# A two-layer hybrid encoder trunk: adaLN sums by one accumulating VectorE operation, a tile-by-tile prologue and transposed host layouts

## The chip, the core and the metric

The kernel runs on one core of a Trainium2 chip. The metric is the device time of one execution in microseconds (us), as the median of several runs. Engines: TensorE (PE in the profile; PEld is its weight load), VectorE (DVE), ScalarE (ACT), GpSimd (POOL), SyncE (SP, which issues most of the DMAs).

## What is computed

The sizes are 1024 tokens, model width 1024, two layers, all in fp32. Cut to what matters here:

```python
def adaln(c, w, b):                       # c (1, 1024), w (1024, 3072)
    mod = (c @ w + b)[:, None, :]
    shift, scale, gate = jnp.split(mod, 3, axis=-1)
    return shift, scale, gate

for l in range(DEPTH):
    shift, scale, gate = adaln(c, w_ada_mix[l], b_ada_mix[l])
    u = x * (1.0 + scale) + shift
    y = hybrid_mixer(u, ...)              # input projection, conv group and attention group, output projection
    x = layer_norm(DN_ALPHA * x + (1.0 + gate) * y, ln1_g[l], ln1_b[l])
    shift, scale, gate = adaln(c, w_ada_ffn[l], b_ada_ffn[l])
    u = x * (1.0 + scale) + shift
    y = conv_gated_mlp(u, ...)            # up, depthwise conv of 3 on the gate branch, SiLU, down
    x = layer_norm(DN_ALPHA * x + (1.0 + gate) * y, ln2_g[l], ln2_b[l])
```

The mixer's conv group is a gated causal depthwise convolution of 31 taps; its attention group has 8 query heads, 2 key heads and a window of two chunks of 64 tokens.

## The kernel before, in words

**Layout.** Activations lie with features on the 128 partitions and tokens along the row: `x` is 8 tiles of 128 features by 1024 tokens. The tokens are worked in two blocks of 512 (T), b = 0 and 1. Every projection is a list of slabs (`SLABS`): one slab makes 128 output features of one block of 512 tokens from 8 (or 5, 6) tiles of 128 inputs. Each fp32 product is made of three reduced-precision ones: the weights are split into `w_hi` (ACT, `split_hi`, L1163) and `w_lo` (POOL, `split_lo`, L1932, four pieces), the inputs into `u_hi` and `u_lo` (or `h_hi`, `h_lo`), and L886 to L888 issue hi x hi, hi x lo and lo x hi. A slab of 8 tiles is 24 matmuls of 512 columns. Kinds of slabs: g, a (conv group), q, k, v (attention), o (output projection), ug, uv (up: gate and value), d (down), e (the last down slabs, second half of the tokens).

**Order.** All engines walk the same list of slabs, and `plan()` hangs small steps on slabs (`STEPS[n]`): conv taps on DVE ("tap"), the attention's scores, maxima, exponentials, turns and weighing of v ("sc", "mx", "pr", "tr", "pv"), the norms ("xm" and so on), the adaLN sums ("ad", "as"), the turning of x ("xt") and of the finished half ("tm"). A planner gives every slab room for DVE steps in tenths of a microsecond (`room`, `used`) and puts the taps where room is left. Slab n's output bank is one of two PSUM banks up to slab 35, one of three from there on; it is freed by ACT or DVE. Weights are loaded four slabs ahead (`NRAW`), split three ahead (`NHI`). On DVE, a ug slab runs two gate operations (L1896, L1899), then the first background step of its list, then the tanh operation (L1905) and the rest of the list; a uv slab runs value times gate (L1912), the first step if the next slab is a ug, `h_lo` (L1919), and the rest. ACT runs, in a uv slab, `h_hi`, `split_hi` and its steps in the order of the list: "mx" makes the exponentials (L1283), "tr" the copy of the turned weights (L1299), for which PE's weighing of v ("pv", L1006) waits.

**Prologue.** x arrives with tokens on the partitions; PE turns it (`x_to_features`, L842, eight 128x128 turns for 128 tokens) and ACT copies it out (`evac_x`, L1168): four tiles before the first slab, four ("xt") behind slabs 2 to 5. The first layer's shift and scale (chunks 0 to 3 of 512 columns) are made in front of the slabs: DVE adds 7 of 8 input tiles weighted by c (`add_first`, L1464, L1467), PE adds the last one and sums over the partitions (`first_sums`, L1093, L1100), in two halves: features 0 to 511 first, then slabs 0 and 1 run over tiles 0 to 3, then the other half. `idle_products` (L1080) fill PE's gaps. POOL makes `u_lo` of tiles 0 to 3 (L2008), DVE that of tiles 4 to 7 (L1519). POOL also makes the angles of the rotary tables in two parts (`angles`, L1948 to L1958).

**adaLN sums of chunks 4 to 23.** A chunk is 512 of the 3072 columns of one of the four adaLN products; a part is a quarter of its 1024 inputs (512 KB). `load_ada` on SP loads one part a step ahead into one of two buffers, when the part before the last is used. Chunks 8, 9 and 10: DVE weights and adds (`add_ada`, L1585, L1588). All others: ACT weights (`ada_scale`, L1324, 2 operations a part) and POOL adds (L1999, L2003). Then PE sums over partitions: chunks 4 to 7 with products against ones (L1018), copied out by ACT; chunks 8 to 23 by turning four blocks (`sum_ada`, L915), reduced by DVE (L1595).

**End.** The first block's finished x is turned by PE in four steps "tm" on slabs 346 to 352 (eight turns each), copied out by ACT and DVE (L1331, L1709), and stored as rows; the second block goes through `tail_turn`, whose norm is made with tokens on the partitions.

## Time and profile before

| | |
|---|---|
| median of 3 runs | 2101.79 us (2101.77 to 2103.06) |
| the profiled execution | 2101.31 us, its span 2099.5 us |
| granted TensorE clock | 0.997 of full speed |
| busy: PE, PEld, DVE, ACT, POOL | 98%, 81%, 57%, 49%, 67% of the span |
| DMA | 250 MB, mean 119 GB/s |

How to read it: a busy share is an average over stages with different limits. Matmuls are pipelined and their ends are modelled, so matmuls overlap in the timeline: the distance from one start to the next is what one costs, and 512 columns are started every 0.227 us in the full stretch. A timeline row gives start, duration, engine, line, operation, output<-inputs, and in brackets the idle time before and what ended it.

### The profile page before, as it was taken

How to read it: one execution, taken by the hardware profiler on the slowest of the kernel's cores; microseconds unless marked ns; L12 is line 12 of the kernel's file. 1: busy time of each engine (PE TensorE's matmuls, PEld its weight loads, DVE VectorE, ACT ScalarE, POOL GpSimd, SP SyncE). 2: the span in 40 equal slices, each digit the busy share in tenths (PEclk: the TensorE clock that was granted, in tenths of full speed). 3: DMA queues.
4: the chain of work that ended last, by engine and by line, in shares of the span. 5: the costliest groups of instructions: out<-in, count | busy, mean ns of one | idle time of the engine just before them, and what ended most of it. 6: DMA issues, size and time to landing. Idle time of an engine off the chain costs nothing.

```text
span 2099.5 us, 27374 instructions
## 1 busy us (share of the span) xinstructions
PE 2064.8 (98%) x9619; PEld 1701.8 (81%) x9619; DVE 1191.1 (57%) x1940; ACT 1031.2 (49%) x1845; POOL 1413.6 (67%) x1780
## 2 busy tenths in 40 slices
PE   7999999999999999999999999999999999999997
PEld 6877778787888878888788888888878888888887
DVE  5888888675515554777632645587651455332235
ACT  3585356555516674374643756235562465333332
POOL 4987767755778887875557885564556776545454
PEclk9999999999999999999999999999999999999999
DMA  8644544533434354553233333332323332434332
GB/s 301 157 134 148 161 127 148 162 108 103 121 111 124 107 162 145 141 159 93 76 100 106 111 111 91 101 103 73 100 76 107 88 104 84 128 99 123 94 100 78
DMA packets 421510, 250.07 MB, mean 119 GB/s; under 512 B 48149, under 2 KB 393085, under 8 KB 421373
## 3 DMA queue, kind: packets, MB, share of 16 engines
q1 hardware_dynamic: 420506, 248.03, 39.8%
q8 instruction: 77, 1.26, 0.3%
q14 instruction: 60, 0.49, 0.1%
q10 hardware_dynamic: 867, 0.29, 0.1%
HBM read 242.71 MB, written 4.26 MB: 118 GB/s over the span
## 4 chain that ended last, share of the span: by engine, by line
PE 86%; POOL 5%; ACT 3%; DVE 3%; issue 2%; ACTq 0%; DMA 0%; POOLq 0%; DVEq 0%
PE fg L886 27%; PE fg L888 27%; PE fg L887 27%; POOL w_lo L1932 3%; PE bank_s L984 1%; POOL ada_acc L2003 1%; ACT ada L1324 1%; PE bank_l L915 1%; PE bank_t L993 1%; PE bank_t L1006 1%; DVE bank_c L1539 0%; POOL ssum L2030 0%; POOL u_lo L2012 0%; ACT probs L1291 0%; ACT probs L1283 0%
## 5 line engine op out<-in xcount | busy, mean ns | idle before, releaser
L1932 POOL TENSOR_TENSOR w_lo<-raw,w_hi 128x256 fp32r<-128x256 f32 (+1 forms) x1425 | 1031.3, 755 | 609.8 <-ACT w_hi L1163 608.7
L886 PE MATMUL fg<-u_hi,w_hi 128*128 128x512 f32 x2112 | 834.7, 395 | 6.2 <-DVE u_lo L1519 2.6
L888 PE MATMUL fg<-u_hi,w_lo 128*128 128x512 f32 x2112 | 823.7, 390 | 0.0
L887 PE MATMUL fg<-u_lo,w_hi 128*128 128x512 f32 x2112 | 823.5, 390 | 0.0
L1163 ACT ACTIVATE w_hi<-raw 128x1024 fp32r<-128x1024 f32 (+2 forms) x387 | 375.6, 971 | 385.6 <-PE fg L888 278.4
L886 PEld LDWEIGHTS fg<-u_hi,w_hi 128*128 128x128 f32 x2112 | 397.1, 188 | 102.5 <-issue 14.5
L888 PEld LDWEIGHTS fg<-u_hi,w_lo 128*128 128x128 f32 x2112 | 397.0, 188 | 84.2
L887 PEld LDWEIGHTS fg<-u_lo,w_hi 128*128 128x128 f32 x2112 | 397.4, 188 | 80.1 <-issue 0.5
L1539 DVE SCALAR_TENSOR_TENSOR bank_c<-glu,par,bank_c 128x512 f32<-128x512 f32 x448 | 306.1, 747 | 0.1
L1886 DVE SCALAR_TENSOR_TENSOR x<-fg,mod,x 128x512 f32<-128x512 f32 (+1 forms) x168 | 121.6, 724 | 319.3 <-PE fg L888 319.0
L888 PE MATMUL fg<-h_hi,w_lo 128*128 128x512 f32 (+1 forms) x704 | 269.8, 383 | 0.0
L886 PE MATMUL fg<-h_hi,w_hi 128*128 128x512 f32 (+1 forms) x694 | 268.4, 387 | 0.6 <-DVE h_lo L1919 0.6
L887 PE MATMUL fg<-h_lo,w_hi 128*128 128x512 f32 (+1 forms) x694 | 266.9, 385 | 0.0
L1896 DVE SCALAR_TENSOR_TENSOR fg<-gate,par,fg 128x512 f32<-128x512 f32 x88 | 66.4, 755 | 331.8 <-ACT fg L1382 331.7
L888 PEld LDWEIGHTS fg<-h_hi,w_lo 128*128 128x128 f32 x704 | 132.3, 188 | 26.0
L886 PEld LDWEIGHTS fg<-h_hi,w_hi 128*128 128x128 f32 x694 | 130.4, 188 | 26.4 <-DVE h_lo L1919 1.0
L887 PEld LDWEIGHTS fg<-h_lo,w_hi 128*128 128x128 f32 x694 | 130.4, 188 | 25.5
L1392 ACT ACTIVATE h_hi<-fg 128x512 fp32r<-128x512 f32 x88 | 52.6, 597 | 175.6 <-DVE fg L1912 175.3
L2003 POOL TENSOR_TENSOR ada_acc<-ada_acc,ada 128x512 f32<-128x512 f32 x102 | 133.2, 1305 | 5.9 <-ACT ada L1324 1.9
L1324 ACT ACTIVATE ada<-ada,ccol 128x512 f32<-128x512 f32 x136 | 90.2, 713 | 5.9 <-DMA ada<-in_w_ada_mix_dram 4.9
L1387 ACT ACTIVATE tanh_c<-fg 128x512 f32<-128x512 f32 x88 | 52.7, 599 | 66.6 <-DVE fg L1899 66.6
L1912 DVE SCALAR_TENSOR_TENSOR fg<-fg,tanh_c 128x512 f32<-128x512 f32 x88 | 61.3, 696 | 42.2 <-PE fg L888 40.3
(272 smaller groups left out, 1860.8 us busy)
## 6 DMA issues: line engine op xcount, KB each, us to landing
raw<-in_w_up_dram SPq DMA_DIRECT2D x176, 512.0 KB, 3.8
ada<-in_w_ada_ffn_dram SPq DMA_DIRECT2D x48, 512.0 KB, 4.4
raw<-in_w_down_dram SPq DMA_DIRECT2D x64, 384.0 KB, 3.5
raw<-in_w_in_dram SPq DMA_DIRECT2D x40, 512.0 KB, 4.0
raw<-in_w_down_dram SPq DMA_DIRECT2D x64, 320.0 KB, 3.1
ada<-in_w_ada_mix_dram SPq DMA_DIRECT2D x32, 512.0 KB, 4.2
raw<-in_w_in_dram SPq DMA_DIRECT2D x32, 256.0 KB, 3.7
raw<-in_w_out_dram SPq DMA_DIRECT2D x32, 256.0 KB, 2.9
```

What stands on the lines that cost most here:

```text
L886: pe.matmul(out, hi[:, k, :], rhi, start=k == order[0], stop=False)
L887: pe.matmul(out, hi[:, k, :], rlo, start=False, stop=False)
L888: ins = pe.matmul(out, lo[:, k, :], rhi, start=False, stop=k == order[-1])
L1163: act.activation(hi_of(n)[:, 0:nk, :], raw[n % NRAW][:, 0:nk, :], ACT.Copy).then_inc(hi_ready, 1)
L1324: act.activation(ada[m % 2][:, i, :], ada[m % 2][:, i, :], ACT.Copy, scale=ccol[:, k:k + 1]).then_inc(ada_mul, 1)
L1387: act.activation(tanh_c[:], ps[:], ACT.Tanh, scale=0.5).then_inc(gate_act, 1)
L1539: ins = dve.scalar_tensor_tensor(out=conv[:, j, :] if k == CONV_K - 1 else acc[:], in0=src, scalar=w, in1=acc[:], op0=ALU.mult, op1=ALU.add)
L1886: dve.scalar_tensor_tensor(out=xs(b, k)[:, cols], in0=ps[:, 0:cols.stop - cols.start], scalar=at_gate, in1=xs(b, k)[:, cols], op0=ALU.mult ...
L1896: dve.scalar_tensor_tensor(out=ps[:], in0=gate[:, 1:1 + T], scalar=par3[:, l, i + FT:i + FT + 1], in1=ps[:], op0=ALU.mult, op1=ALU.add).th ...
L1912: dve.scalar_tensor_tensor(out=ps[:], in0=ps[:], scalar=0.5, in1=tanh_c[:], op0=ALU.mult, op1=ALU.mult).then_inc(gate_dve, 1)
L1932: ins = pool.tensor_tensor(lo_of(n)[:, ks, :], raw[n % NRAW][:, ks, :], hi_of(n)[:, ks, :].bitcast(F32), ALU.subtract)
L2003: pool.tensor_tensor(acc[:], acc[:], rows[:, i, :], ALU.add).then_inc(ada_add["pool"], 1)
```

## The change

1. **Host layouts.** x comes transposed (1024 features by 1024 tokens) and is loaded straight into `x`; the first block's result is stored straight from `x` (`out_t`, features by tokens) and transposed on the host; the adaLN weights come transposed, so that 128 adaLN columns lie on the partitions and the 1024 inputs along the row (`ada_first`, `ada_t`). The turns of x ("xt", "tm"), their copies and `stage_in` are gone.
2. **c as rows.** PE spreads c over all partitions (two products against ones), ACT copies it to `c_rows` (128x1024).
3. **adaLN sums.** One 128x1024 operation with an accumulated output makes one column of `mod`, for 128 adaLN columns. First chunks: sixteen on DVE (`first_total`). Chunks 8, 9, 10 and 12 to 23: one on DVE for each part (`ada_total`). Chunks 4 to 7 and 11: POOL multiplies (`ada_weigh`, 2 operations), ACT sums in the next slab, behind its other steps ("ae"). PE's sums, ACT's and DVE's copies of them ("as") and `ada_acc` are gone.
4. **Tile-by-tile prologue.** Loads, sums, gain and bias (now on ACT), `tmp`, `u_hi` (ACT) and `u_lo` (all on POOL) go tile by tile, and slabs 0 and 1 take each tile as it comes. The idle products are gone; the taps' turns stand behind tile 5.
5. **The plan's room** is kept as it was (`used` gets the same amounts; DVE's new operations from chunk 12 on get none beyond the old reduction's), so the taps and norms stand in the same slabs.

The core of the diff:

```diff
-INSIDE = {("cm", 0): 2, ("cv", 0): 4, ("xm", 0): 4, ("xr", 0): 6,
-          ("as", 12): 2, ("as", 18): 2}
+INSIDE = {("cm", 0): 2, ("cv", 0): 4, ("xm", 0): 4, ("xr", 0): 6}
...
-DVE_CHUNKS = (8, 9, 10)
-ONES_CHUNKS = (4, 5, 6, 7)
+DVE_CHUNKS = (8, 9, 10, *range(12, 4 * NCHUNK))
...
         for part, n in enumerate(ns):
             put(n, "ad", c, part)
-            if c in DVE_CHUNKS:
+            if c in DVE_CHUNKS[0:3]:
                 used[n] += 15
-        if c in ONES_CHUNKS:
-            at(ns[-1] + 2, "as", c)
-        else:
-            put(ns[-1] + 2, "as", c)
+        for part, n in enumerate(ns):
+            if c not in DVE_CHUNKS:
+                at(n + 1, "ae", c, part)
+        if c >= DVE_CHUNKS[0]:
+            used[ns[-1] + 2] += 7
...
     for t in range(TB, TT):
-        put(t - TB + 2, "xt", t)
+        used[t - TB + 2] += 7
...
+            def load_x(b, i):
+                sp.dma_start(x[:, 2 * i:2 * i + 2, b * T:(b + 1) * T],
+                             a["x"][2 * i * P:2 * (i + 1) * P, b * T:(b + 1) * T].rearrange("(k p) n -> p k n", p=P)).then_inc(in_x[b][i], 16)
             def load_ada(m):
                 if m >= 2:
-                    sp.wait_ge(ada_add[added(m - 2)[0]], added(m - 2)[1])
+                    sp.wait_ge(*part_done(m - 2))
...
+            for k in range(DT):
+                load_first(k)
+                if k % 2 == 0 and k < DT // 2:
+                    load_x(0, k // 2)
+                if k == 1 or k == 3:
+                    load_w(k // 2)
+                if k == 4 or k == 5:
+                    load_x(0, k - 2)
+                if k == 5:
+                    load_rows(rows2, rows3)
...
+            for half in (0, 1):
+                pe.matmul((bank_t, bank_s)[half][:], ones_1[0:1, :], c_rows[0:1, half, :], start=True, stop=True).then_inc(set_pe, 1)
...
             def first_inputs(k):
+                act.wait_ge(first_one, 1)
+                act.wait_ge(first_sum, 2 * k + 1)
+                act.activation(bias[:, 0, k:k + 1], mod[:, 0, 0, k:k + 1], ACT.Identity,
+                               bias=par1[:, 0, OFF["b_ada_mix"] + k:OFF["b_ada_mix"] + k + 1]).then_inc(first_fold, 1)
+                act.wait_ge(first_sum, 2 * k + 2)
+                act.activation(gain[:, 0, k:k + 1], mod[:, 0, 0, DT + k:DT + k + 1], ACT.Identity, bias=scale_0[:, k:k + 1]).then_inc(first_fold, 1)
+                act.wait_ge(first_fold, 2 * k + 2)
+                if k % 2 == 0:
+                    act.wait_ge(in_x[0][k // 2], 16)
+                if k >= 2:
+                    act.wait_ge(ilo, k - 1)
+                inputs(tmp[:, k % 2, :], xs(0, k), 0, k, iu)
                 inputs(u_hi[0][:, k, :], xs(0, k), 0, k, ihi)
...
+            def ada_total(c, part):
                 m = (c - CHUNKS_BEFORE) * QUARTERS + part
+                act.wait_ge(ada_mul, 2 * sum(ada_engine(i) == "act" for i in range(m + 1)))
+                rows = ada[m % 2][:].rearrange("p h n -> p (h n)")
+                act.activation(rows, rows, ACT.Copy, accum_out=total_of(c, part)).then_inc(ada_done["act"], 1)
...
+            split_hi(0)
             for k in range(DT):
-                if k == DT // 2:
-                    split_hi(2)
+                if k == 2:
+                    split_hi(1)
                 first_inputs(k)
+            split_hi(2)
...
+            def first_total(k, half):
+                dve.wait_ge(in_first[k][half], 16)
+                rows, c = first_ada[k][:, half, :], half * DT + k
+                dve.scalar_tensor_tensor(out=rows, in0=rows, scalar=1.0, in1=c_rows[:].rearrange("p h n -> p (h n)"),
+                                         op0=ALU.mult, op1=ALU.mult, accum_out=mod[:, 0, 0, c:c + 1]).then_inc(first_sum, 1)
...
+            def ada_total(c, part):
                 m = (c - CHUNKS_BEFORE) * QUARTERS + part
                 dve.wait_ge(in_ada[m % 2], 16 * (m // 2 + 1))
+                rows = ada[m % 2][:].rearrange("p h n -> p (h n)")
+                dve.scalar_tensor_tensor(out=rows, in0=rows, scalar=1.0, in1=c_rows[:].rearrange("p h n -> p (h n)"),
+                                         op0=ALU.mult, op1=ALU.mult, accum_out=total_of(c, part)).then_inc(ada_done["dve"], 1)
...
+            def ada_weigh(c, part):
                 m = (c - CHUNKS_BEFORE) * QUARTERS + part
+                pool.wait_ge(in_ada[m % 2], 16 * (m // 2 + 1))
+                pool.wait_ge(set_col, 2)
+                for i in (0, 1):
+                    pool.tensor_tensor(ada[m % 2][:, i, :], ada[m % 2][:, i, :], c_rows[:, i, :], ALU.mult).then_inc(ada_mul, 1)
...
-            for n in range(2):
-                split_lo(n)
-            for k in range(DT // 2):
+            split_lo(0)
+            for k in range(DT):
+                if k == 2:
+                    split_lo(1)
+                if k == 4:
+                    angles(0)
                 first_lo(k)
-            angles(0)
             split_lo(2)
-            pool.wait_ge(set_pe, 4)
+            pool.wait_ge(set_pe, 5)
```

## Rows read from the trace of the kernel before

**Rows 1.** The page: busy us, share of the span and instructions of each engine.

```profile
PE 2064.8 (98%) x9619; PEld 1701.8 (81%) x9619; DVE 1191.1 (57%) x1940; ACT 1031.2 (49%) x1845; POOL 1413.6 (67%) x1780
```

**Rows 2.** Windows: stretch in us, its length, busy us (operations) of each engine, clock, DMA.

```profile
400.00:450.00 50.00, 48.83 (x246) 39.15 (x245) 31.62 (x58) 36.51 (x94) 34.69 (x40) 1.00 0.44 132
```

**Rows 3.** Timeline of PE: a turn of four blocks and the matmuls behind it.

```profile
233.15 0.60 PE L915 MATMUL bank_l<-const,ada_acc 128*128 128x128 f32 x4
233.51 0.48 PE L886 MATMUL fg<-u_hi,w_hi 128*128 128x512 f32 x1
233.82 0.40 PE L887 MATMUL fg<-u_lo,w_hi 128*128 128x512 f32 x1
```

**Rows 4.** Timeline of PE: a turn of x with its next matmul, and a ones sum.

```profile
70.78 0.60 PE L842 MATMUL bank_t<-const,stage_in 128*128 128x128 f32 x4
...
71.57 0.48 PE L886 MATMUL fg<-u_hi,w_hi 128*128 128x512 f32 x1
...
83.45 0.95 PE L1018 MATMUL bank_l<-const,ada_acc 128*128 128x1 f32 x8
84.26 0.49 PE L886 MATMUL fg<-u_hi,w_hi 128*128 128x512 f32 x1
```

**Rows 5.** Timelines of ACT and of SP in the prologue.

```profile
11.42 0.60 ACT L1168 ACTIVATE x<-bank_t 128x512 f32<-128x512 f32 x1
...
27.27 0.80 ACT L1173 ACTIVATE tmp<-x,bias,gain 128x512 f32<-128x512 f32 x1
...
35.25 0.33 SPq L741 DMA_DIRECT2D rows<-in_conv_w_dram  x1
```

**Rows 6.** Timeline of DVE: operations with two inputs in SBUF.

```profile
89.24 1.22 DVE L1660 SCALAR_TENSOR_TENSOR probs<-probs,const,cs 128x512 f32<-128x512 f32 x1
...
237.17 1.89 DVE L1588 SCALAR_TENSOR_TENSOR ada_acc<-ada,ccol,ada_acc 128x512 f32<-128x512 f32 x2
...
279.30 0.75 DVE L1588 SCALAR_TENSOR_TENSOR ada_acc<-ada,ccol,ada_acc 128x512 f32<-128x512 f32 x1
```

**Rows 7.** Timeline of POOL from the angles to the first rope product.

```profile
33.69 0.24 POOL L1948 CAST ang<-pos 128x64 f32<-128x64 int32 x1
...
40.21 3.60 POOL L1932 TENSOR_TENSOR w_lo<-raw,w_hi 128x256 fp32r<-128x256 f32 x4
...
52.40 2.83 POOL L1932 TENSOR_TENSOR w_lo<-raw,w_hi 128x256 fp32r<-128x256 f32 x4 [1.84 <-ACT w_hi L1163]
...
62.60 2.81 POOL L1932 TENSOR_TENSOR w_lo<-raw,w_hi 128x256 fp32r<-128x256 f32 x4 [1.32 <-ACT w_hi L1163]
...
77.47 0.21 POOL L1965 COPY glu<-glu 128x30 f32<-128x30 f32 x1 [1.25 <-DVE conv L1544]
...
80.59 1.30 POOL L1987 TENSOR_TENSOR q<-q,cs 128x512 f32<-128x512 f32 x1
81.84 3.71 POOL L1932 TENSOR_TENSOR w_lo<-raw,w_hi 128x256 fp32r<-128x256 f32 x4
```

**Rows 8.** One turn of the attention loop: timelines of PE, DVE and ACT.

```profile
400.86 0.65 PE L1006 MATMUL bank_t<-probs_t,v 128*64 128x256 f32 x4 [0.62 <-ACT probs_t L1299]
414.21 0.65 PE L1006 MATMUL bank_t<-probs_t,v 128*64 128x256 f32 x4 [0.21 <-ACT probs_t L1299]
...
403.53 0.33 DVE L1693 TENSOR_TENSOR st<-st 128x4 f32<-128x4 f32 x1
406.95 0.42 DVE L1701 TENSOR_TENSOR u_lo<-bank_t,u_hi 128x256 fp32r<-128x256 f32 x1 [1.97 <-ACT u_hi L1305]
408.60 0.69 DVE L1912 SCALAR_TENSOR_TENSOR fg<-fg,tanh_c 128x512 f32<-128x512 f32 x1
409.20 0.68 DVE L1683 TENSOR_REDUCE st<-bank_s 128x4 f32<-128x512 f32 x1
...
405.38 1.27 ACT L1291 ACTIVATE probs<-probs,st 128x128 f32<-128x128 f32 x4
412.00 0.35 ACT L1283 ACTIVATE probs<-bank_s,st 128x128 f32<-128x128 f32 x1
```

More of the change, by code:

```diff
@@ L484, in build @@
         ada = [sb(f"ada{i}", [P, 2, T]) for i in range(2)]
-        ada_acc = [sb(f"ada_acc{i}", [P, T]) for i in range(2)]
+        c_rows = sb("c_rows", [P, 2, T])
         tmp = sb("tmp", [P, 2, T])
@@ L655, in spread_before, with part_done, total_of @@
             return (cstat if kind == "c" else xstat), 3 * (i + 1)
-        def copied(c):
-            return (ada_copied, c - CHUNKS_BEFORE + 1) if c in ONES_CHUNKS else (ada_reduced, c - ONES_CHUNKS[-1])
+        def part_done(m):
+            e = ada_engine(m)
+            return ada_done[e], sum(ada_engine(i) == e for i in range(m + 1))
+        def total_of(c, part):
+            l, ffn, j = c // NCHUNK // 2, c // NCHUNK % 2, c % NCHUNK
+            return mod[:, l, ffn, j * TB + part:j * TB + part + 1]
         def tmp_free(turn):
@@ L1008, in weigh_v @@
                 ins.then_inc(pv_done, 1)
-            def sum_ada(c):
-                e, adds = added((c - CHUNKS_BEFORE + 1) * QUARTERS - 1)
-                pe.wait_ge(ada_add[e], adds)
-                take(SUM_BANK[c], *copied(c))
-                out = bank_t if SUM_BANK[c] == "t" else bank_l
-                src = ada_acc[c % 2]
-                if c in ONES_CHUNKS:
-                    for i in range(TB):
-                        ins = pe.matmul(out[:, i:i + 1], src[:, i * P:(i + 1) * P], ones_1[:, 0:1], start=True, stop=True)
-                    ins.then_inc(ada_sum, 1)
-                else:
-                    turned(out, lambda i: src[:, i * P:(i + 1) * P]).then_inc(ada_sum, 1)
-            def to_tokens(t, half, out):
-                ins = transposes(out, half, lambda k: x[:, k, t * P:(t + 1) * P])
-                ins.then_inc(y_t_done, 1)
             def do(step):
@@ L1820, in background @@
                 elif what == "ad":
-                    add_ada(*step[1:])
-                elif what == "as" and step[1] not in ONES_CHUNKS:
-                    reduce_ada(step[1])
+                    ada_total(*step[1:])
                 elif what == "fold":
@@ L2120, in _, with ada_engine @@
             pool.tensor_tensor(stage_out[2][:, 0:T], stage_out[2][:, 0:T], b_rows[:, 0:T], ALU.add).then_inc(y_pool, 1)
-def added(m):
-    engines = ["dve" if CHUNKS_BEFORE + i // QUARTERS in DVE_CHUNKS else "pool" for i in range(m + 1)]
-    e = engines[m]
-    return e, sum(2 - (e == "pool" and i % QUARTERS == 0) for i in range(m + 1) if engines[i] == e)
+def ada_engine(m):
+    return "dve" if CHUNKS_BEFORE + m // QUARTERS in DVE_CHUNKS else "act"
 TAIL_SMALL, TAIL_SMALL_2 = 12, 5
```

348 lines of the change are left out of this document (72 added, 276 removed).

## The prediction, as made before the result

> **What bounds the kernel now.** I read the page's busy shares first: TensorE (PE) works 2064.8 of 2099.5 us [rows 1], so the end is set by PE's own work and by the few places where PE starts late or waits. The windows come next: in a stretch with attention, 400 to 450 us, PE is busy 48.8 of 50 while VectorE (DVE) has 31.6 of 50 [rows 2]. So PE is full and DVE seems to have room; whether it has it where it is asked is the question of this change. Then the timelines of PE around the operations that go [rows 3, 4], those of the start [rows 5, 7], and one turn of the attention loop on all engines [rows 8].
>
> The program's 2101.3 us are the span of 2099.5 and 1.8 around it, and lie 0.5 below the median of the three runs, 2101.79. I sum against 2101.3. Differences of about 0.2% (4 us) can't be told from no change.
>
> **Work taken off PE in its full stretch (after about 110 us).**
> (1) The sums of chunks 8 to 23 turned four 128x128 blocks each. One set starts at 233.15, the next matmul at 233.51, and the one behind that after 0.31 instead of 0.23 [rows 3]: 0.36 + 0.08 = 0.44 us; by the 16 chunks of the code: 7.0 us. None lies beside other work of PE.
> (2) Chunks 5, 6 and 7 used ones: 83.45 to 84.26, and again 0.08 [rows 4], 0.9 each: 2.7 us. Chunk 4 and the turns of x in the four slabs behind the prologue (70.78 to 71.57 plus 0.08: 0.87 us each [rows 4]) go too, but lie before 110 us, where I find another bound (below): nothing.
> (3) The step "tm" turns a finished 128-token tile in eight turns, as the turn of x does: 4 x 0.87 = 3.5 us.
> Sum 13.2 us. What PE did to wait for these sums goes as well; I count 0.5. Together 13.7.
> The output's stores leave straight from x while PE goes on; ScalarE (ACT) and DVE lose their copies. If those stores were late they would have some 200 us until the end. Nothing.
>
> **The prologue.** Removed: the turns of x, the idle products, DVE's 28 weighted sums and its u_lo. Added: two broadcasts of c on PE and two copies on ACT; sixteen DVE operations of 128x1024 with a sum; u_lo of all eight tiles on GpSimd (POOL); the two angle tables' first part now between tile 3 and tile 4 on POOL. ACT's first computation stood at 11.42, behind its DMA issues and a table load [rows 5]; c_rows comes out of two such copies, so DVE begins at about 12.6 where it used to begin at 7.9.
> What one of the sixteen costs has no row. A 128x512 operation with both inputs in SBUF took 0.75 us with POOL quiet, and a pair of them 1.89 with POOL at work; one such of the rope took 1.22 [rows 6]. Twice the width pays the fixed part once: below 2 x 0.75 = 1.5, above 1.2; with the reading of the sum I take 1.35 quiet, and 2.1 beside a busy POOL (1.9 to 2.4). POOL pays too: its four pieces of w_lo took 3.71 us beside such operations instead of 2.8 [rows 7].
> Sixteen at 1.35 are 21.6 us, so alone they would end at 34; with some 15 us of POOL work in the same stretch they end at 40 to 42. The loads let the last tile land at about 35 (the queue's wait for the last adaLN piece ended at 35.25 [rows 5]), since the same 11 MB come before it. But POOL and ACT have their own chain, because tmp has two slots: tile k waits for u_lo of tile k-2. POOL runs w_lo twice (2.8 each), u_lo 0 to 3 (1.3 each, as the same shape in [rows 7]), then the angles, which took 33.69 to 40.21, 6.5 us [rows 7], then u_lo 4 to 7, where tile 6's two ACT operations (0.7 to 0.8 each [rows 5]) wait for u_lo 4. First inputs start when DVE has two tiles, at about 19; this chain gives 19 + 2 + 2 x 1.3 + 2.8 + 2 x 1.3 + 6.5 + 2 x 1.3 + 2 + 2 + 1.3 = 43.4, and 47 with the contention. So w_lo of slab 2 starts at 43.5 to 47 instead of 40.21 [rows 7].
> From there on POOL was nearly never idle until 80.59: it waited 1.84, 1.32 and 1.25 us, and lost 0.8 in the first slab's pieces [rows 7]. In the changed kernel these waits go, because PE's first two slabs end only 1.5 to 3 us after tile 7 instead of 8 us after tile 4. Chunk 4 gives POOL one more operation of 1.3. Balance at 80.59: +3.3 to +6.8 later start, -5.2, +1.3: between 0.6 earlier and 2.9 later. POOL's chain (a rope product 1.3, w_lo 3.7 and a u_lo 1.3 in each slab [rows 7], 6.3 us against PE's 24 x 0.227 = 5.5) then leads to the first scores; PE's turns of x that are gone don't show there. I take 1 us later. **Prologue: +1.0** (from -3 to +6).
> PE's low clock there costs nothing more as long as POOL is what it waits for.
>
> **ACT and POOL, chunks 4 to 7 and 11.** POOL weighs, ACT sums one step later: ACT 1.2 for 1.4, POOL 8 for 7 operations. A load now waits for ACT's sum, which is last in its slab. The two buffers turn once in two slabs (11 us): load 4.4, POOL's turn and ACT's take it up nearly whole. POOL prepares weights three slabs ahead, so a lateness of 2 to 3 us is hidden: nothing, at worst 2.
>
> **DVE from chunk 12 on.** 48 operations of 128x1024 replace 84 on POOL, 96 on ACT, and 12 reductions on DVE (chunks 8 to 10: 12 for 24 of about 0.95 each, no change worth counting). As DVE load that is 48 x 1.7 = 82 less 8 us, and hidden on the average. The planner counts none of it (used[n] gets only the 7 of the old reduction), and "ad" stands first in a slab's list. Where the slab is an up slab, the first background step runs between the two gate operations and the tanh one, and where it is a value slab, before h_lo. In chunks 13 and 14 (slabs 56 to 63) and 22 (158 to 161, with 21's end) this pushes "pr" and "mx" of the attention behind it.
> One turn of this loop, gate slab and value slab, took from 400.86 to 414.21, 13.35 us [rows 8], in step with PE, which had hardly waited. I follow it with two new operations a1 and a2. From the weighing of v to the second gate operation's end 2.67 (400.86 to 403.53); a1; tanh operation 0.6 (as 408.60 to 409.20); "pr" 0.55; normalise and u_hi up to DVE's u_lo 1.57 (405.38 to 406.95); u_lo and two taps 1.65 (to 408.60); value times gate 0.6; a2; h_lo 0.6; maxima 1.0 (0.68 and two small ones); exponentials, copy of the turned weights, up to the next weighing 2.2 (412.00 to 414.21) [rows 8]. Sum 11.45 + a1 + a2. a1 meets w_lo on POOL: 2.1. a2 comes before that slab's w_lo: 1.35. Turn: 14.9, 1.55 more than now. Four such turns in chunks 13 and 14: 6.2. In mixer 2, slabs 158/159 have no u_lo yet but PE's turn of the weights waits: some 1.9; 160/161 1.55. Two of the removed 0.44 lie in turns that PE no longer sets: 0.9. **Together 10.5**; with a1 = a2 = 1.3 it would be 4, with 2.4 and 2.1 some 17. Break-even is a1 + a2 = 1.9.
> Elsewhere (down, g and a slabs, the norms) DVE may fall behind by 2 to 3 us and catch up, with three banks between it and PE. For small waits there I add 1.
>
> **Sum:** 2101.3 - 13.7 + 1.0 + 10.5 + 1.0 = 2100; PE waits less than this where the loop has been drawn too strictly, so I take the rounding down: **2099.0**, own range 2093 to 2106.
>
> **Rivals.**
> (B) The operation hides. POOL has lost its sums, so contention is short, a1 and a2 are both near 1.3, the loop costs 4, and the prologue gains 2 to 3: 2101.3 - 13.7 + 4 - 2.5 = 2089. For it: DVE's 31.6 of 50 [rows 2], and that 1.9 of the loop is free. Against it: at 403.53 DVE's new operation falls just where POOL's w_lo runs. 0.29.
> (C) Slower: the accumulating operation with two SBUF inputs streams at half rate, 2.5 to 2.7 us. Sixteen take 42 us, the prologue is 13 us late, and a turn of the loop takes 11.45 + 5.7, 3.8 more, by 5.5 turns 21: 2101.3 - 13.7 + 13 + 21 = 2122. It decides from about 1.9 us quiet on. Against it: the one with 0.75 us for 512 columns [rows 6] had two SBUF inputs and full rate; for it: no row has a sum written out. 0.10.
> The Trainium skill (Vector Engine (DVE) Microarchitecture Reference, section "Points that are easy to get wrong") says that an operation of this family with two SBUF sources that aren't bf16 runs at half throughput. By that rule the time would be that of C; the trace disagrees for the form without the sum.
> (D) Slower in part: the prologue's chain of ACT and POOL through two slots of tmp, with DVE and POOL blocking each other, ends at 52 instead of 46: 2106. It decides where the last u_lo comes after 48. 0.14.
> The Trainium skill (SBUF — State Buffer, section "Who interferes with whom") has DVE and GpSimd exclude each other for a whole instruction when DVE has two SBUF inputs. By that rule a1 would be 1.35 and at most one piece of w_lo, as above, and the prologue's DVE and POOL work would lie end to end, which leads to D; the rows show both slowed by about a third to a half.
> Forecast 0.47.
>
> **How the numbers follow.** Faster by over 0.2% (under 2097.6): B and two fifths of the forecast, 0.46. Within: three fifths of the forecast and half of D, 0.35. Slower (over 2106.0): C, half of D and 0.02, 0.19. Range 2087 to 2110: it leaves out C and the outer part of B.
>
> **What would show it.** Right: DVE's new operation about 1.35 us with POOL idle and near 2 beside w_lo; turns of the loop of 14.5 to 15.3 us with PE waiting for ACT's copy of the turned weights; PE waits of 8 to 12 us in slabs 56 to 64 and 158 to 162; no turns of sums; first scores about 1 us later than now. Wrong: first scores over 3 us earlier or over 4 later, an operation of 2.6 us, turns of 13.4 us, or waits of PE for data of the sums' loads.

## The result, and the profile after

The changed kernel takes 2122.3 us (median of four runs, 2117.5 to 2128.2) where the kernel before takes 2101.8 (four runs, 2101.6 to 2103.1): a ratio of 1.0097, 95% interval 1.0069 to 1.0126. I had forecast 2099 with a range of 2087 to 2110 and 0.19 for slower, so the prediction was wrong. The spread is news as well: 10.7 us between its runs against 1.5 before. The profiled execution took 2124.7 us, its span 2122.9.

The page of the changed kernel, busy time and the costliest group of the new operation:

```profile
PE 2038.3 (96%) x9288; PEld 1671.4 (79%) x9288; DVE 1243.6 (59%) x2008; ACT 969.3 (46%) x1747; POOL 1353.0 (64%) x1705
...
L1422 DVE SCALAR_TENSOR_TENSOR ada<-ada,c_rows 128x1024 f32<-128x1024 f32 x60 | 82.3, 1372 | 9.0 <-DMA ada<-in_ada_t_dram 9.0
```

PE has 26.5 us less to do than in [rows 1] and yet ends 23.4 us later, so some 50 us are idle time that the kernel before did not have, or had less of. Who made PE wait, longest in total first (engine, line, releaser: us in total, times, longest):

```profile
PE fg L849 <- POOL w_lo L1741: 31.1, 8, 18.7
PE bank_t L969 <- ACT probs_t L1191: 7.4, 7, 1.7
PE bank_s L947 <- DVE kz L1502: 6.3, 1, 6.3
...
PE bank_t L956 <- ACT probs L1183: 4.6, 2, 3.2
```

Of the first, 18.7 us are the start of the program and 8.4 come at slab 10, behind DVE's long operation that is shown below; the second is the attention loop of my forecast; the other two I had not expected. To place the loss in time I read, for every slab, when the first w_lo of its weights is loaded into PE, and subtract the kernel before's time for the same slab. This table is worked out from the traces and is the ruler of all that follows. "pauses", "last" and "psum" are kernels of the experiments below, each with all edits of the one before it.

```
slab   before   |  after   pauses  +last   +psum    (us later than before)
0        29.9   |   6.1     6.3     5.9    -2.6
2        51.7   |   5.0     5.0     6.0    -6.6
9        95.5   |   1.7     5.7     6.4    -6.0
11      109.8   |  17.7     9.2     9.9    -2.2
12      116.6   |  18.1    10.3    11.3    -1.2
23      195.8   |  16.9     9.4    10.4    -2.0
33      257.0   |  22.6    14.4    12.9     0.1
47      341.5   |  21.3    14.1    12.7    -0.1
48      348.7   |  24.2    13.7    12.3    -0.6
56      381.8   |  23.8    13.1    11.8    -1.1
65      442.1   |  29.4    18.8     9.9    -3.0
158     911.0   |  24.6    13.9     4.6    -8.2
200    1132.8   |  27.5    16.8     3.3    -9.5
346    1872.1   |  27.1    16.4     2.9   -10.0
360    1935.6   |  23.5    12.8    -0.7   -13.5
```

The column "after" has five features: 16.0 us lost between slabs 9 and 11, 5.7 between 23 and 33, 3.0 at slab 48, 5.7 in the first attention loop (56 to 65) and 2.9 in the second (158 to 200); and gains of 4.9 (65 to 158) and 3.6 (346 to 360).

**Slabs 9 to 11 and slab 48.** DVE's timeline (start, us, engine, line, operation, idle before it):

```profile
85.53 12.93 DVE L1488 SCALAR_TENSOR_TENSOR probs<-probs,const,cs 128x512 f32<-128x512 f32 x1 [0.79 <-DMA probs<-q]
98.38 0.74 DVE L1378 TENSOR_SCALAR bank_c<-glu,par 128x512 f32<-128x512 f32 x1
...
358.39 6.18 DVE L1513 SCALAR_TENSOR_TENSOR st<-st,nsink 128x4 f32<-128x4 f32 x1
```

The same rope operation took 1.22 in [rows 6], the one on 128x4 elements 0.28 in the kernel before. While the first lasted, POOL did this:

```profile
84.79 2.54 POOL L1805 TENSOR_TENSOR ada<-ada,c_rows 128x512 f32<-128x512 f32 x2
87.29 1.29 POOL L1796 TENSOR_TENSOR q<-q,cs 128x512 f32<-128x512 f32 x1
88.53 2.83 POOL L1741 TENSOR_TENSOR w_lo<-raw,w_hi 128x256 fp32r<-128x256 f32 x4
91.32 1.30 POOL L1814 TENSOR_TENSOR u_lo<-tmp,u_hi 128x512 fp32r<-128x512 f32 x1
92.57 1.31 POOL L1796 TENSOR_TENSOR q<-q,cs 128x512 f32<-128x512 f32 x1
93.82 2.85 POOL L1741 TENSOR_TENSOR w_lo<-raw,w_hi 128x256 fp32r<-128x256 f32 x4
96.59 1.32 POOL L1814 TENSOR_TENSOR u_lo<-tmp,u_hi 128x512 fp32r<-128x512 f32 x1
```

Each row of POOL begins where the last one ends, and all of them run at their quiet durations (four pieces of w_lo 2.83, against 3.71 beside DVE in [rows 7]). DVE's operation ends 0.55 us after POOL's last one. So it was kept out for 14 operations of POOL in a row: I call such an operation caught. The first product of the rope is [rows 7]'s 80.59, now 87.29, and behind the catch come the swaps' DMAs, the sums of the rope, kz and the first scores. PE then also starts slowly, with 0.43 us from matmul to matmul, where the last two rows are 0.24 apart and the ones behind them 0.23:

```profile
111.05 0.79 PE L849 MATMUL fg<-u_hi,w_hi 128*128 128x512 f32 x1 [8.44 <-POOL w_lo L1741]
111.64 0.63 PE L850 MATMUL fg<-u_lo,w_hi 128*128 128x512 f32 x1
...
114.20 0.59 PE L850 MATMUL fg<-u_lo,w_hi 128*128 128x512 f32 x1
114.63 0.40 PE L851 MATMUL fg<-u_hi,w_lo 128*128 128x512 f32 x1
114.87 0.40 PE L849 MATMUL fg<-u_hi,w_hi 128*128 128x512 f32 x1
```

The reason is the granted clock, which the share of 0.992 for the whole span hides. It was at half (1.2 of 2.4 GHz) from 107.8 to 114.6 us, while and after PE waited those 8.44 us. Windows of the changed kernel (stretch, length, busy us and operations of PE, PEld, DVE, ACT and POOL, clock, DMA share, GB/s):

```profile
107.80:114.60 6.80, 3.55 (x8) 2.81 (x9) 6.80 (x9) 2.60 (x3) 6.80 (x8) 0.50 0.43 121
...
223.90:227.20 3.30, 3.30 (x10) 2.53 (x9) 2.16 (x5) 2.92 (x5) 0.02 (x1) 0.50 0.00 0
275.10:278.40 3.30, 3.30 (x9) 2.59 (x8) 3.11 (x6) 2.39 (x4) 1.08 (x1) 0.50 0.02 5
```

It was at half again from 121.4 to 128.3 and from 442.3 to 445.7. The profile of the kernel before has full clock from 48.2 to 2092.8. Where PE has work through such a stretch of 3.4 us, it gets through 1.7 us less of it.

**The prologue.** POOL's timeline, to be laid beside [rows 7]:

```profile
18.22 6.08 POOL L1741 TENSOR_TENSOR w_lo<-raw,w_hi 128x256 fp32r<-128x256 f32 x4 [17.78 <-ACT w_hi L1060]
24.27 4.44 POOL L1810 TENSOR_TENSOR u_lo<-tmp,u_hi 128x512 fp32r<-128x512 f32 x2
28.67 6.70 POOL L1741 TENSOR_TENSOR w_lo<-raw,w_hi 128x256 fp32r<-128x256 f32 x4
35.33 4.48 POOL L1810 TENSOR_TENSOR u_lo<-tmp,u_hi 128x512 fp32r<-128x512 f32 x2
39.77 0.23 POOL L1757 CAST ang<-pos 128x64 f32<-128x64 int32 x1
...
51.19 1.28 POOL L1810 TENSOR_TENSOR u_lo<-tmp,u_hi 128x512 fp32r<-128x512 f32 x1 [0.65 <-ACT u_hi L1064]
52.42 2.12 POOL L1741 TENSOR_TENSOR w_lo<-raw,w_hi 128x256 fp32r<-128x256 f32 x3
```

The four stretches beside DVE's sums took 21.7 us where the same work takes 10.6 quiet. The last u_lo starts at 51.19 and w_lo of slab 2 at 52.42, not at 43.5 to 47.

**The attention loop.** DVE around the two new operations of one turn:

```profile
435.06 1.22 DVE L1422 SCALAR_TENSOR_TENSOR ada<-ada,c_rows 128x1024 f32<-128x1024 f32 x1
436.20 0.08 DVE L1422 DVE_READ_ACCUMULATOR ada<-ada,c_rows 128x1 f32 x1
436.20 0.69 DVE L1728 TENSOR_TENSOR h_lo<-fg,h_hi 128x512 fp32r<-128x512 f32 x1
436.80 0.68 DVE L1511 TENSOR_REDUCE st<-bank_s 128x4 f32<-128x512 f32 x1
...
443.89 1.37 DVE L1422 SCALAR_TENSOR_TENSOR ada<-ada,c_rows 128x1024 f32<-128x1024 f32 x1
```

PE's weighing of v at the end of the first turn:

```profile
426.23 0.65 PE L969 MATMUL bank_t<-probs_t,v 128*64 128x256 f32 x4 [1.71 <-ACT probs_t L1191]
```

The new operation stands where I had put it, ahead of h_lo and the maxima, and costs 1.2 to 1.4 us there. From one weighing of v to the next, which is how the forecast counted, the four turns took 15.3, 15.0, 15.0 and 14.4 us, where the kernel before has 13.7, 13.4, 13.9 and 13.1. PE waited for ScalarE's copy of the turned weights at the end of the first and second (1.71 and 1.75 us) and of the fourth (1.12). In the third it waited only 0.26, but the half clock of 442.3 to 445.7 falls into it.

### The profile page after: what moved, and what is told of

It is laid out like the page before. It is cut to its first block, busy times and chain, and to the rows that moved or that the text cites. A ratio compares the mean times of both kernels' runs of the same rounds, so it can differ in the third digit from the quotient of the medians.

```text
span 2122.9 us, 26513 instructions
## 1 busy us (share of the span) xinstructions
PE 2038.3 (96%) x9288; PEld 1671.4 (79%) x9288; DVE 1243.6 (59%) x2008; ACT 969.3 (46%) x1747; POOL 1353.0 (64%) x1705
## 3 DMA queue, kind: packets, MB, share of 16 engines
q8 instruction: 74, 1.21, 0.2%
## 4 chain that ended last, share of the span: by engine, by line
PE 79%; DVE 8%; POOL 6%; ACT 3%; issue 2%; DMA 1%; ACTq 0%; SPq 0%; POOLq 0%; DVEq 0%
PE fg L849 25%; PE fg L850 25%; PE fg L851 25%; POOL w_lo L1741 3%; DVE bank_c L1381 1%; DVE ada L1422 1%; PE bank_s L947 1%; DVE probs L1488 1%; ACT probs L1175 1%; DVE st L1513 1%; POOL u_lo L1810 0%; PE bank_t L969 0%; POOL ada L1805 0%; DVE fg L1705 0%; DVE fg L1708 0%
## 5 line engine op out<-in xcount | busy, mean ns | idle before, releaser
L1741 POOL TENSOR_TENSOR w_lo<-raw,w_hi 128x256 fp32r<-128x256 f32 (+1 forms) x1425 | 1062.3, 776 | 690.7 <-ACT w_hi L1060 690.2
L1422 DVE SCALAR_TENSOR_TENSOR ada<-ada,c_rows 128x1024 f32<-128x1024 f32 x60 | 82.3, 1372 | 9.0 <-DMA ada<-in_ada_t_dram 9.0
L1728 DVE TENSOR_TENSOR h_lo<-fg,h_hi 128x512 fp32r<-128x512 f32 x88 | 60.5, 688 | 25.1 <-ACT h_hi L1270 24.2
```

The lines of the kernel that those rows point to most:

```text
L1422: dve.scalar_tensor_tensor(out=rows, in0=rows, scalar=1.0, in1=c_rows[:].rearrange("p h n -> p (h n)"), op0=ALU.mult, op1=ALU.mult, accum_ ...
L1728: dve.tensor_tensor(h_lo[:, k, :], ps[:], h_hi[:, k, :].bitcast(F32), ALU.subtract).then_inc(freed["dve"], 1)
L1741: ins = pool.tensor_tensor(lo_of(n)[:, ks, :], raw[n % NRAW][:, ks, :], hi_of(n)[:, ks, :].bitcast(F32), ALU.subtract)
```

## The experiments

Each kernel was timed beside the kernel before on the same chip; that one's median was 2102.3 to 2103.2 in the four groups. Lines of code are those of the changed kernel.

### Is it the same again, and what do pauses of GpSimd do?

The changed kernel once more:

> The changed kernel once more, unchanged. Theory S (a DVE operation with two inputs in SBUF is kept waiting while GpSimd runs without a pause): whether it is caught depends on where in GpSimd's sequence it arrives, so the time again spreads by several us (2115 to 2129), and the profile again shows one or two such operations of over 5 us, not necessarily the same ones. Theory D (the late prologue by itself pushes everything back): time within 2 us of 2122, every run alike.

Measured: 2124.4 (2113.1 to 2125.4, 4 runs). The rope operation took 1.21 us this time, and two others were caught:

```profile
140.42 9.10 DVE L1521 TENSOR_TENSOR st<-st 128x4 f32<-128x4 f32 x1
```

and the small one at slab 46 again, for 6.16. So where an operation is caught changes from run to run, and so does the time.

Then one line more for GpSimd, a wait for its own product:

```
 for i in (0, 1):
     pool.tensor_tensor(ada[m % 2][:, i, :], ada[m % 2][:, i, :], c_rows[:, i, :], ALU.mult).then_inc(ada_mul, 1)
+    pool.wait_ge(ada_mul, <count of this product>)
```

> One edit to the changed kernel: GpSimd waits for each of its two products c x piece before it goes on, 78 ns or so each, as the kernel before did through its accumulation. Theory S: the rope operation at slab 5 to 9 takes under 2.6 us instead of 12.93, no small operation takes over 2 us, first scores come 14 to 18 us earlier, and the 16 us between slab 9 and slab 11 go, as do the 3.0 at slab 48: about 2105, 2102 to 2108, and its runs spread by under 3 us. Theory D: the sums' prologue stays late, so 2120 to 2124.

Measured: 2114.3 (2111.2 to 2115.5, 5 runs), ratio 1.0048 (1.0035 to 1.0060). No operation is caught; the rope operation took 1.49:

```profile
86.08 1.49 DVE L1488 SCALAR_TENSOR_TENSOR probs<-probs,const,cs 128x512 f32<-128x512 f32 x1 [1.19 <-DMA probs<-q]
```

The 3.0 at slab 48 is gone and the spread is 4.2 us. But only 8 to 10 us are won, not 16 to 19: the table has 10.3 us at slab 12 with the pauses. The catch came on top of a prologue that was late already; without it that lateness shows. Both theories had a part of the truth, and my expectation gave the catch too much.

### Where in DVE's list do the sums stand?

```
 if n < LAST_BEAT:
     mine.sort(key=lambda step: step[0] == "pv")
+if n >= POS["d", 0, 0, (0, 0)]:
+    mine.sort(key=lambda step: step[0] == "ad")
```

> The same with the pauses, and DVE makes its adaLN sum of a slab last of its background steps from slab 48 on (chunks 12 to 23) instead of first. If the sums stand in the way of the attention loop (5.7 us lost from slab 57 to 65 and 2.9 from 158 to 170), these go: 6 to 9 us less than with the pauses alone, about 2098. If the loop is late for another reason (DVE's load as such, or the two inputs that it shares with GpSimd), within 2 us of the kernel with the pauses alone.

Measured: 2102.2 (2099.3 to 2103.2, 11 runs), ratio 0.9994 (0.9985 to 1.0003): 12.1 us less than with the pauses alone. In the table the 5.7 us of slabs 56 to 65 become a gain of 1.9, and the 2.9 of slabs 158 to 200 a gain of 1.3. That is more than the 6 to 9 us that I expected, and the two rows of the table make 11.8 of it. The turns of the first loop now took 13.04 us each, and PE did not wait for ScalarE in them. The loss was the place of the operation in the list, not DVE's load: the number of operations is the same.

The other way to take the sums out of the loop is to undo DVE's part, `DVE_CHUNKS = (8, 9, 10)`:

> The same with the pauses, and chunks 12 to 23 made as chunks 4 to 7 and 11 are: GpSimd multiplies, ACT sums one slab later. It undoes DVE's part alone. If DVE's operation costs what the landmarks say (5.7 + 2.9 us in two attention loops), and GpSimd hides its 96 products as it did before, 7 to 9 us less than with the pauses alone, about 2097. If the products of GpSimd keep DVE's operations waiting, or ACT's sums come into the way of the loop's exponentials, less is gained: 2 to 5 us, or a loss.

Measured: 2107.0 (2104.5 to 2111.0, 11 runs), 7.3 us less than with the pauses alone. In the first loop it is as good as the sums last (9.5 against 9.9 us late at slab 65); from slab 80 to 300 it falls from 9.1 to 7.7 where that one falls from 9.4 to 2.9, with PE waiting 3.8 us in all for DVE's h_lo. DVE's operation is the better one if it stands last.

### What sets the first scores?

On the kernel with the pauses and the sums last. First, GpSimd's angle table ahead of everything (the edit also puts the load of the constants that it reads on the semaphore of c, not shown; DVE's first sum still started at 12.9 us):

```
+angles(0)
 split_lo(0)
 for k in range(DT):
     if k == 2:
         split_lo(1)
-    if k == 4:
-        angles(0)
     first_lo(k)
```

> The pauses and the adaLN sums last, as before, and GpSimd makes the first angle table (7.5 us, at 39.58 to 47.08) ahead of its first piece of w_lo, where it idled to 19.2 us; the small constants that it needs count on the semaphore of c. Theory G (from 19 us to the first scores GpSimd is never idle, so its work and nothing else sets their time): w_lo of slab 2 starts at 46 to 47 instead of 53.27, the first product of the rope 6 to 7.5 us earlier than at 89.48, slab 12 at about 121 instead of 127.8, time 6 to 7 us less: 2095 to 2096. Rival (DVE's sums, the loads or PE's first two slabs set it): w_lo of slab 2 moves, but slab 12 by under 2 us, 2100 to 2102.

Measured: 2099.2 (2095.0 to 2101.4, 11 runs), 3.0 us less. w_lo of slab 2 moved from 53.27 to 49.74 only: beside DVE's sums the angles lasted from 11.61 to 25.94, 14.3 us instead of 7.5, and put off w_lo of slab 0; slab 12 came 3.1 us earlier. GpSimd's work does count, but moving it under the same contention buys half of what I expected.

Second, c is read where TensorE made it. bank_t and bank_s become the halves of one PSUM tensor of 1024 columns, and

```
-in1=c_rows[:].rearrange("p h n -> p (h n)"),
+in1=pair[:],
```

in the prologue's sums only:

> The pauses and the sums last, and DVE's sixteen sums of the prologue read c in the PSUM banks where TensorE made it, not from SBUF: each of them then has one input in SBUF. Theory P (the two engines take turns at the SBUF inputs, which costs GpSimd 3.1 us in each of the first two slabs' w_lo and 0.95 in each of four u_lo, 9.8 in all): w_lo of slab 0 takes 2.8 us instead of 5.88, u_lo 1.3 instead of 2.2, a sum 1.15 to 1.25 us throughout; w_lo of slab 2 starts 7 to 9 us earlier, and the time falls by 6 to 9 us to 2093 to 2096. Rival (the sums wait for their loads anyway, and GpSimd then waits for the sums): the pieces get short, but GpSimd idles between them, and the time falls by under 3 us.

Measured: 2091.0 (2087.4 to 2093.2, 5 runs), ratio 0.9943 (0.9930 to 0.9955): 11.2 us less, where I expected 6 to 9. All sixteen sums took 1.22 us, and POOL runs at its quiet pace beside them:

```profile
L1329 DVE SCALAR_TENSOR_TENSOR first_ada<-first_ada,pair x16: 1215/1220/1222, 12.9 to 37.0; 128x1024 f32<-128x1024 f32 x16
```

```profile
18.66 2.79 POOL L1744 TENSOR_TENSOR w_lo<-raw,w_hi 128x256 fp32r<-128x256 f32 x4 [18.22 <-ACT w_hi L1061]
21.40 2.51 POOL L1814 TENSOR_TENSOR u_lo<-tmp,u_hi 128x512 fp32r<-128x512 f32 x2
23.86 2.79 POOL L1744 TENSOR_TENSOR w_lo<-raw,w_hi 128x256 fp32r<-128x256 f32 x4
26.60 2.54 POOL L1814 TENSOR_TENSOR u_lo<-tmp,u_hi 128x512 fp32r<-128x512 f32 x2
...
41.77 2.84 POOL L1744 TENSOR_TENSOR w_lo<-raw,w_hi 128x256 fp32r<-128x256 f32 x4
```

w_lo of slab 2 starts at 41.77 instead of 53.27. The first row's columns are duration in ns (least, median, most) and first and last start. With c in SBUF, in the changed kernel, the same row had 1217, 1730 and 2289. That is the prologue's whole loss: one input of sixteen operations. The Trainium skill (SBUF — State Buffer, section "Who interferes with whom") says that a VectorE instruction with at most one SBUF input does not contend with GpSimd, outside of some modes. By that rule these sums would leave POOL alone; the trace agrees.

Both edits together:

> Both of the last two edits together. If GpSimd's work sets the first scores, the two add until the loads' landing (about 36 us) or the kernel before's start of slab 2 at 40 sets it: w_lo of slab 2 at 39 to 42, slab 12 at 114 to 117, time 2090 to 2093. If they hit the same bound behind, it is no better than the better of the two alone.

Measured: 2091.0 (2088.8 to 2091.2, 5 runs). No better than the second alone: without contention GpSimd idles 4.41 us before the u_lo of tile 6, for ACT, which waits for DVE's sums, and DVE waited 4.9 us for the loads of `ada_first`. ScalarE's order was the last try in the prologue, the first slab's weights split before par1 is copied:

> c from PSUM, pauses, sums last, and ScalarE splits the first slab's weights before it copies par1, for whose rows it waited 4.0 us. GpSimd's first w_lo starts at about 14 us instead of 18.66. If GpSimd's work still sets the first scores, 2 to 3 us less (2088 to 2089); if since the contention is gone the landing of the last adaLN piece (37 us) and the chain of ACT behind it set slab 2, nothing, within 1 us of 2091.

Measured: 2090.4 (2086.6 to 2092.1, 5 runs), the same as 2091.0, the second of the two cases: w_lo of slab 0 started at 15.03 instead of 18.66, and w_lo of slab 2 at 41.91 as before.

One more on slab 24, the sums last from slab 23 on, with c in SBUF:

> The pauses, and the sums last from slab 23 on, chunks 8 to 10 too (before, they stood first there). In slab 23 DVE waited 4.07 us for a load of chunk 8 with the conv norm's steps queued behind it, and PE waited 2.8 for their end. If that head-of-line wait is the loss at slab 24 (1.7 us in this kernel), the time is 1.5 to 2.5 us under the kernel with the sums last from slab 48: about 2100. If the norm would be late anyway, the same within 1 us; and if chunk 10's late sums hold up their loads and with them the weights queued behind, 1 to 3 us more.

Measured: 2100.9 (2098.4 to 2103.6, 11 runs) against 2102.2, intervals that overlap (0.9981 to 0.9998, and 0.9985 to 1.0003). But this run does not test what it was made for. The sum in DVE's way is the first one of chunk 8, and it stands in the list of slab 22, ahead of the conv norm's steps; the edit begins with slab 23, which has no sum at all. So the wait was still there, first in the changed kernel, then in this run:

```profile
217.03 1.33 DVE L1422 SCALAR_TENSOR_TENSOR ada<-ada,c_rows 128x1024 f32<-128x1024 f32 x1 [4.07 <-DMA ada<-in_ada_t_dram]
...
222.68 0.66 PE L878 MATMUL bank_l<-const,wide 128*128 128x128 f32 x4 [2.83 <-DVE wide L1416]
```

```profile
210.63 1.56 DVE L1422 SCALAR_TENSOR_TENSOR ada<-ada,c_rows 128x1024 f32<-128x1024 f32 x1 [5.47 <-DMA ada<-in_ada_t_dram]
...
216.93 1.07 PE L878 MATMUL bank_l<-const,wide 128*128 128x128 f32 x4 [4.52 <-DVE wide L1416]
```

The loss at slab 24 can be read in this place. From the end of PE's sums for the norm to its turn of `wide` the kernel before took 3.6 us (200.1 to 203.6), the changed one 5.7 (217.0 to 222.7) and this one 7.4: 2.2 and 3.9 us more, where the table has 2.1 and this run 4.1 from slab 23 to 24. Of this, 1.3 and 2.6 us are the time from PE's sums until the adaLN sum at the head of the list was done, 0.9 each the four operations that make `wide`, which took 1.83 and 1.86 instead of 0.93. The kernels with the pauses and with the sums last are the same up to slab 48, and lost 4.1 and 1.7 there, so the amount changes from run to run. The rest of the 5.7 us up to slab 33 lies mostly in the two stretches of half clock shown above (1.7 us each) and in a wait of 1.99 us at 274.1 for GpSimd's ssum. That these waits go if the sum of slab 22 is moved was not tried.

### What catches an operation?

First the reverse test, on the kernel before:

```
-pool.wait_ge(ada_add["pool"], n - 2 + i)
-pool.tensor_tensor(acc[:], acc[:], rows[:, i, :], ALU.add).then_inc(ada_add["pool"], 1)
+pool.tensor_tensor(rows[:, i, :], rows[:, i, :], rows[:, i, :], ALU.add).then_inc(ada_add["pool"], 1)
```

> The kernel BEFORE with GpSimd's pauses taken away: its additions to ada_acc, each of which waits for the one before, are replaced by as many additions of the same size within the loaded piece, which wait for nothing; this leaves out three quarters of the adaLN sums of chunks 4 to 7 and 11 to 23. Theory S: the kernel before was safe only because of these pauses, so here too one or more DVE operations with two SBUF inputs are caught for 5 to 13 us, and the time is 3 to 12 us above the kernel before, with a wider spread. Rival (the long operations belong to the changed kernel: its reads of c_rows, its later prologue): no such operation, within 1.5 us of the kernel before.

Measured: 2099.5 (2098.2 to 2102.1, 11 runs), ratio 0.9987 (0.9978 to 0.9996). Nothing with two SBUF inputs was caught, and the time did not rise, so the theory as I had put it falls. But one operation of another kind was held in the same way, one with a single tensor input on 128x4 elements:

```profile
1175.04 4.45 DVE L1570 TENSOR_SCALAR small<-small 128x4 f32<-128x4 f32 x1
```

It came while GpSimd was in a piece of w_lo, and ended 0.02 us after the sixth operation of GpSimd, the last before a pause. The quickest of this line took 0.17. Even the kernel before has a stretch of 35 us without a pause, from 79.0 on, in which DVE's operations with two SBUF inputs got their turn behind one or two operations of GpSimd.

Then three kernels without pauses, with the sums last and c in PSUM:

> c read from PSUM in the prologue and the sums last, without the pauses between GpSimd's products. Theory S: whether an operation is caught depends on the moment when it arrives, so between nothing (2091, as with the pauses) and 10 us more (2101), with a spread of over 5 us; the profile shows a caught operation only if its run was long. Rival (the pauses help through something else, such as the order of GpSimd's work): a steady 5 to 8 us more than 2091 in every run.

Measured: 2098.2 (2087.0 to 2108.4, 12 runs), against 2091.0 and a spread of 5.8 with the pauses. The rope operation was caught again:

```profile
74.50 12.92 DVE L1489 SCALAR_TENSOR_TENSOR probs<-probs,const,cs 128x512 f32<-128x512 f32 x1 [0.84 <-DMA probs<-q]
```

> As the last one, and GpSimd multiplies a piece by c in one operation of 1024 columns instead of two of 512: no pauses, but no two products in a row either. If a DVE operation is caught only where it arrives in the first of two products that follow each other without a wait, none is caught here: 2090 to 2092. If any stretch of GpSimd without a pause can catch one, as in the kernel without the pauses, up to 10 us more; a DVE operation that meets the long product waits up to 2.5 us for it, which costs 1 to 3 us in the attention loops.

Measured: 2092.6 (2091.2 to 2098.7, 5 runs), with one caught:

```profile
337.88 5.76 DVE L1514 SCALAR_TENSOR_TENSOR st<-st,nsink 128x4 f32<-128x4 f32 x1
```

so one long product catches as two short ones do, at the same place in the program.

> No pauses, and the two inputs of GpSimd's products change places (c_rows first, the piece second). All six caught operations had arrived in a product of the piece with c_rows, none of some 2000 that arrived in another operation of GpSimd with two SBUF inputs and none behind it. If it is that operation's order of operands, none is caught: 2089 to 2092. If not, as without the pauses: median 2094 to 2100, runs up to 2108.

Measured: 2096.7 (2086.6 to 2107.9, 12 runs), with one caught for 9.10 us at 129.54. The order of the inputs is not it.

Last, one pause instead of two, between the products:

> c from PSUM, sums last, and GpSimd pauses only between its two products of a piece, not behind them. In the profiles so far every one of the six caught DVE operations had arrived during the first of two products (or the only one). Theory F (the first product with the next behind it is what catches): none is caught, 2089 to 2092 with a spread under 6 us. Rival (any product on c_rows without a pause behind it catches): the second still does, about 2095 with runs up to 2105.

Measured: 2088.9 (2087.5 to 2091.0, 5 runs), ratio 0.9933 (0.9921 to 0.9945), nothing caught. And one behind them:

> As the last one, with the pause only behind the second product. If an operation that is caught comes free at the next pause, wherever that is, one that arrives in the first product waits for two at most (2.6 us): 2090 to 2093, spread under 6 us, and no operation over 3.2 us. If it takes a pause at the first boundary to keep it from being caught at all, about 2098 as with no pause.

Measured: 2090.4 (2087.6 to 2091.0, 5 runs), ratio 0.9939 (0.9927 to 0.9950), nothing caught. Either pause was enough.

What the traces have in common: the five profiles of the four kernels that form these products without pauses (the changed one twice) hold seven caught operations. All seven arrived while GpSimd was in a product of an adaLN piece with c_rows; none was caught in ten profiles of kernels with pauses. Nor was one among the thousand or so DVE operations with two SBUF inputs that arrived in another operation of GpSimd in the same five profiles. This holds like for like too: where GpSimd went on for over 4 us without a pause, 7 of 35 arrivals in a product were caught and none of 275 in its other operations. All sit at three places (the first rope operation, and the attention's small ones at slabs 13 and 46). What makes this product different stays open, and so does whether the 4.45 us at 1175, which came in a piece of w_lo, are the same thing. That no operation was caught once GpSimd paused between the two products or behind them is shown. What the pause is worth depends on the kernel: 8 to 10 us of the changed one and most of its spread, 7 to 8 with c in PSUM, about 6 with the inputs swapped, 2 to 3 with the one long product.

## Why the prediction was wrong, step by step

Two steps failed. The prologue, put at +1.0 us, priced the contention for DVE and hardly for GpSimd: it was 10.3 us late at slab 12 even with the pauses. And the wait that the change took from GpSimd was put at nothing: without it DVE's operations were caught, which cost 8 to 10 us. A third, smaller one is "nothing, at worst 2" for chunks 4 to 10, which came to 7.5.

**PE's work after 110 us, 13.2 us: right.** Where nothing else moves, the table falls by 0.49 for a turn of four blocks (slabs 85 to 89, 111 to 115), by 0.8 to 0.9 for a ones sum (slabs 15 and 19), and by 3.57 in slabs 346 to 360 for the four steps "tm". That makes 7.8 + 2.6 + 3.6 = 14.0.

**The attention loop, 10.5 us: right in mechanism and size.** From 56 to 65 the table rises by 5.7, from 158 to 200 by 2.9; with the removed turns in these stretches, one and two of 0.49, that is 10.1. The first four turns were longer than before by 1.6, 1.6, 1.1 and 1.3 us, where I had 1.55 for each. The parts came out otherwise: a1 was 1.37 rather than 2.1 where it is shown. PE's waits in these slabs came to 8.7 us (8 to 12 forecast), 7.1 of them for ScalarE's copies of the turned weights.

**DVE's new operation: right.** 1.22 us quiet against 1.35 forecast, 1.7 to 2.3 in the prologue beside POOL against 2.1. Rival C, half rate, falls. The Trainium skill (Vector Engine (DVE) Microarchitecture Reference, section "Points that are easy to get wrong") gives half throughput for such an operation with two SBUF sources that aren't bf16; here 1024 columns took the same 1.22 us with one and with two inputs in SBUF, so the measurement speaks against the rule for this shape.

**The prologue, +1.0 us: the term that failed.** "This chain gives ... 43.4, and 47 with the contention": I gave POOL 3.6 us for it, and it was 11.1 (21.7 for 10.6). I had priced what DVE's operations lose to POOL, sixteen times, and for POOL only the [rows 7] figure of 3.71 for 2.8, taken where DVE had a single such operation now and then. Here DVE had sixteen in a row without idle time, so each of POOL's pieces waited for most of one: 1.66 us from start to start instead of 0.70. The way back was better than I had it (5.5 us of the lateness regained by the first rope product; forecast were 5.2 less 1.3 for the added operation), so 6.7 us were left there (8.2 in the profile with the pauses), and 10 at slab 12. In the profile with the pauses the granted clock was at half from 94.0 to 97.4 and from 114.5 to 121.3, which is part of the last 2. This is rival D's mechanism, with its condition (last u_lo after 48) met at 51.2, and its price too small: 2106 was 7 us over the forecast, and the one input in SBUF was worth 11.2.

**What no rival had: the catch.** In the profiled run it cost 7.8 at slab 12 (18.1 against 10.3 with the pauses) and 3.0 at slab 48; over the runs 8 to 10 us. My costs of an operation beside POOL ended at 2.4 us, from rows in which one side waits for one operation of the other, and the change took a wait from GpSimd that I had priced at nothing and had not looked at as a protection.

**Chunks 4 to 7 and 8 to 10, "nothing, at worst 2": too low.** 5.7 us from slab 23 to 33, or 7.5 with the removed sums (0.8 + 2 x 0.49). The step that failed is "12 for 24 of about 0.95 each, no change worth counting": the number of operations is no matter, but the first sum of chunk 8 waited 4.07 us for its load at the head of DVE's list and held up the norm's steps behind it by 1.3 us, PE waited 2.83 us for them and 1.99 for GpSimd's ssum, and the clock fell to half behind each of the two waits. This is read from the traces; no run takes it away.

The sum with the measured terms: 2101.3 - 14.0 + 10.1 + 10.3 (slab 12, pauses) + 7.8 + 3.0 + 7.5 = 2126, against 2124.7 in the profiled execution.

## What to carry to other kernels

If the Vector engine and GpSimd work at the same time, count an operation's inputs in SBUF on both sides: where Vector has no gaps, price each operation of GpSimd at nearly the two together (1.66 and 2.20 us here, where the sums are 1.85 and 2.40), and look whether one of the inputs already lies in PSUM. Put a long filler operation last in a slab's list, behind the steps that other engines wait for. And when a change removes a wait or lets an engine run without pauses, look afterwards at the longest single operations of the other engine, not at their means, and at the spread of the runs. Where PE starts late, read the granted clock of the stretch as well as the wait.

The fastest kernel of the study by its median has three edits on the changed one: c from PSUM in the prologue, the sums last from slab 48, a pause between GpSimd's two products. It takes 2088.9 us, 0.67% less than the kernel before, where the change alone took 0.97% more. The five kernels with c from PSUM and a pause lie within 2.2 us and their intervals overlap, so they can't be ranked.

## What the runs showed of the hardware

- An operation of VectorE with two SBUF inputs can be held for 13 us behind 14 operations of GpSimd, and one on only 128x4 elements for 9.1 us behind 10. The Trainium skill (SBUF — State Buffer, section "Summary: rules for kernel authors") has the one that issues second fully block until the first finishes, where VectorE has two SBUF inputs and GpSimd's operation reads SBUF; the seven caught operations waited for 5 to 14 of them, so here the wait is not bounded by one.
- Two streams without gaps take turns operation by operation: DVE's sums and POOL's pieces of w_lo both came 1.66 us apart, where alone they come 1.15 and 0.70 apart, and 2.20 beside u_lo, which alone comes 1.25 apart.
- An input in PSUM instead of SBUF costs the operation nothing (1.22 us either way), and GpSimd beside it ran at its quiet pace (four pieces of w_lo in 2.79 us, 6.08 to 6.70 with both inputs in SBUF).
- PE waited 8.44 us, from 102.6 to 111.0; the granted clock was 0.50 from 107.8 to 114.6, and the matmuls came 0.43 us apart until then and 0.23 afterwards: some 1.6 us on top of the wait itself. Shorter waits were followed by half clock too: 2.83 us (half from 223.8 to 227.3), 1.99 us (275.0 to 278.5) and 1.75 us (442.3 to 445.7).
